# The chunk scan of a state-space layer on VectorE alone, in a one-core decoder step

## The reference, cut to what matters

```python
x_re = jnp.einsum('bngc,gpc->bngp', ug, bb_re)      # and x_im
combine: (a2r*a1r - a2i*a1i, a2r*a1i + a2i*a1r,
          a2r*b1r - a2i*b1i + b2r, a2r*b1i + a2i*b1r + b2i)
_, _, s_re, s_im = lax.associative_scan(combine, (l_re, l_im, x_re, x_im), axis=1)
y = einsum(s_re, c_re) - einsum(s_im, c_im)
```

## Time and profile before

| | |
|---|---|
| median of 3 runs | 2636.78 us |
| lowest and highest run | 2634.36 and 2637.1 us |
| profiled execution, first to last instruction (span) | 2638.2 us |
| mean granted TensorE clock | 0.945 of full speed |
| TensorE matmuls busy | 2385.0 us (90%) |
| VectorE busy | 1067.1 us (40%) |
| ScalarE busy | 816.8 us (31%) |
| GpSimd busy | 221.8 us (8%) |

### The profile page before, as it was taken

How to read it: one execution, slowest core, us unless ns; L and a number is a source line. 1 busy time by engine, 2 the same in 40 slices (tenths; PEclk the granted TensorE clock), 3 DMA queues, 4 the chain that set the end, 5 groups by cost and what they waited for, 6 DMA issues and landing times.

```text
span 2638.2 us, 46341 instructions
## 1 busy us (share of the span) xinstructions
PE 2385.0 (90%) x19286; PEld 2155.6 (82%) x19286; DVE 1067.1 (40%) x1547; ACT 816.8 (31%) x1145; POOL 221.8 (8%) x324
## 2 busy tenths in 40 slices
PE   6999997928998999998899999798996768999999
PEld 5999996724698999998799999754774448999998
DVE  4333324784534433323433332355363222434422
ACT  3443222302323434322334322222343212434311
POOL 2000001363200000000000000000002410000000
PEclk9999997967998999999899999899798988999999
DMA  3323332000032332332233333101003522233332
GB/s 91 96 87 94 102 88 55 1 0 6 2 84 70 88 95 88 104 90 54 66 96 87 95 96 88 33 21 35 11 18 88 156 78 73 72 95 87 101 94 78
DMA packets 361265, 188.87 MB, mean 72 GB/s; under 512 B 39772, under 2 KB 357338, under 8 KB 361154
## 3 DMA queue, kind: packets, MB, share of 16 engines
q1 hardware_dynamic: 354624, 176.91, 23.5%
q0 software_dynamic: 5104, 8.90, 1.2%
q10 hardware_dynamic: 1426, 1.46, 0.2%
HBM read 184.21 MB, written 3.02 MB: 71 GB/s over the span
## 4 chain that ended last, share of the span: by engine, by line
PE 63%; DVE 4%; SPq 4%; issue 2%; ACT 1%; DMA 0%; POOL 0%; DVEq 0%; ACTq 0%
PE ps L1371 51%; PE ps L1691 2%; PE ps L1380 2%; PE ps L1786 1%; PE ps L1759 1%; SPq L356 1%; SPq L357 1%; SPq L351 1%; DVE ta L917 1%; PE ps L1743 1%; DVE xl L904 1%; PE ps L1589 1%; DVE rstc L1217 1%; PE ps L1393 1%; PE ps L1762 1%
## 5 line engine op out<-in xcount | busy, mean ns | idle before, releaser
L1371 PE MATMUL ps<-xh,wh 128*128 128x260 f32 x3296 | 873.7, 286 | 23.7 <-DVE xl L904 20.9
L1371 PE MATMUL ps<-xl,wh 128*128 128x260 f32 x3296 | 864.5, 284 | 0.0
L1371 PE MATMUL ps<-xh,wl 128*128 128x260 f32 x3296 | 667.4, 284 | 0.0
L1371 PEld LDWEIGHTS ps<-xh,wh 128*128 128x128 f32 x3296 | 627.2, 190 | 32.8 <-issue 20.0
L1371 PEld LDWEIGHTS ps<-xl,wh 128*128 128x128 f32 x3296 | 626.1, 190 | 0.0
L894 DVE TENSOR_TENSOR wl<-raw,wh 128x1024 fp32r<-128x1024 f32 (+1 forms) x208 | 274.6, 1320 | 746.1 <-ACT wh L536 746.1
L1371 PEld LDWEIGHTS ps<-xh,wl 128*128 128x128 f32 x3296 | 512.2, 190 | 0.0
L536 ACT ACTIVATE wh<-raw 128x1024 fp32r<-128x1024 f32 (+1 forms) x208 | 236.5, 1137 | 662.6 <-PE ps L1371 662.6
L1371 PE MATMUL ps<-hh,wh 128*128 128x260 f32 x1408 | 370.4, 284 | 0.0
L1371 PE MATMUL ps<-hl,wh 128*128 128x260 f32 x1408 | 367.4, 282 | 0.0
L1371 PE MATMUL ps<-hh,wl 128*128 128x260 f32 x1408 | 283.3, 282 | 0.0
(11 more groups left out here) (348 smaller groups left out, 2429.0 us busy)
## 6 DMA issues: line engine op xcount, KB each, us to landing
raw<-ffn_w_gate SPq DMA_DIRECT2D x88, 512.0 KB, 3.9
raw<-ffn_w_up SPq DMA_DIRECT2D x88, 512.0 KB, 3.9
raw<-ffn_w_down SPq DMA_DIRECT2D x64, 704.0 KB, 4.6
cb<-cache_ckv SPq DMA_DIRECT2D x72, 128.0 KB, 2.5
cb<-cache_ckv POOLq DMA_DIRECT2D x56, 128.0 KB, 2.6
raw<-s_w_glu_v SPq DMA_DIRECT2D x8, 512.0 KB, 4.1
raw<-s_w_glu_g SPq DMA_DIRECT2D x8, 512.0 KB, 4.0
raw<-mla_w_o SPq DMA_DIRECT2D x8, 512.0 KB, 4.0
```

Of the source, the lines that this page charges most:

```text
L1371: got = mm(ps[0:width, bank + half, 0:HALF], w[par_][:, k * width:k * width + width], src[:, k0 + k, half * HALF:half * HALF + HALF], star ...
```

## The change

GpSimd no longer scans any pairs. VectorE scans all 32 pairs in one call, with the same 21 steps of four instructions, each now twice as wide. GpSimd's wait for tile 3 is gone with its scan, and it goes from `mu` directly to the wait for all tiles and the sample tokens' step. VectorE's waits and the semaphore counts stay as they are.

```diff
-SCAN_T = 4
...
             dve.wait_ge(s_mu, 1)
             dve.wait_ge(s_xe, KD)
-            chunk_scan(own, tt, pr, QP * SCAN_T, NPAIR, s_sn)
+            chunk_scan(own, tt, pr, 0, NPAIR, s_sn)
...
             pool.wait_ge(s_mu, 1)
-            pool.wait_ge(s_xe, SCAN_T)
-            chunk_scan(own, T, gtmp, 0, QP * SCAN_T)
-
-
             pool.wait_ge(s_xe, KD)
             pool.wait_ge(s_ev, 1)
```

## The result

| | before | after |
|---|---|---|
| median of 14 runs each | 2636.94 us | 2646.41 us |
| lowest to highest | 2634.36 to 2640.81 | 2639.85 to 2650.24 |
| profiled execution: device time, span | – , 2638.2 | 2641.32, 2639.7 |

The ratio is 1.003, 95% interval 1.002 to 1.0039: 7.9 us slower (5.3 to 10.3), where 8.7 was forecast. The medians alone are 9.5 apart. The runs of one kernel lie 6 to 10 us apart, so the stage is read from the traces and the total from the medians.

The account below looks back on a forecast made before the run. VectorE's scan was taken to bound the state-space stage, its end carrying over one to one. Start 539.7 + scan 59.1 + contention 3.6 = 602.4 against 593.7, 8.7 us later: 2645.5 us, range 2640.5 to 2652.0.

Parts of the forecast that it names:

- The loop: Input loop: without GpSimd's scan the tiles keep 10.05 us and VectorE's scan starts 6.5 us earlier, at 539.7.
- the 7.5 of TensorE alone: Input loop: the bound if TensorE's time alone set the scan's start, 538.7 instead of 546.2.
- The width: VectorE's scan: 6.35 ns per element of a step, steps of 3.90, 1.05 and 3.49 us, 59.1 us in all.
- Rival A: VectorE's scan: extra elements cost only the contiguous 1.04 ns, scan ends at 594.1, no change, or 586.5 if stronger; 5%.
- The contention: Start of VectorE's scan: GpSimd's sample step now runs beside the first two steps and costs them 3.6 us.
- B: Start of VectorE's scan: the sample step hides without loss, 5.1 us later in all, 2641.9 us; 7%.
- C: Start of VectorE's scan: full blocking by GpSimd's sample step, 6.7 us instead of 3.6, 2648.6 us; 10%.
- What costs nothing: GpSimd's sample step ends at about 546, more than 50 us before the scan ends, so its lateness is covered.
- The clock: TensorE's granted clock, rising in the first taps: unchanged place, 0 us; bounds 2.5 saved to 9 more.
- a later stage getting shorter would prove it wrong: Stages behind the scan: a later one that shortens by what the scan lost would make the prediction wrong.

Follow-up runs that it names:

- e1: Kernel before, with GpSimd's half scan waiting for all eight tiles instead of tile 3; 2650.11 us in one run.
- e3: Changed kernel without the sample tokens' state step on GpSimd (sn set to zero); scan on VectorE 59.4 us, 2633.43 us in one run.
- v1: Changed kernel with the chunks in xs reordered so the scan walks runs of neighbouring elements; 2644.77 us, 1.0028 to the kernel before.
- e2: Changed kernel with VectorE scanning pairs 16 to 31 alone, pairs 0 to 15 left out; scan 39.7 us, 2617.88 us in one run.
- v6: Kernel before with the sample step's early part moved ahead, contiguous operands in VectorE's scan, and GpSimd scanning 12 pairs from tile 2; 2631.59 us, ratio 0.9976.
- v7: Kernel before with the sample step's early part moved ahead, contiguous operands in VectorE's scan, and GpSimd scanning 8 pairs from tile 1; 2629.32 us, ratio 0.9962.

## Why the prediction was right

Forecast 2645.5 us in a range of 2640.5 to 2652.0, measured 2646.41. The +8.7 us rested on three terms. Each was measured in the changed kernel and again by an edit that makes or removes it alone. The numbers in brackets below are those of the prediction's parts.

| term | forecast | changed kernel | alone |
|---|---|---|---|
| input loop without GpSimd's scan | -6.5 | -6.5 (52.1 to 45.5) | -6.5 (e1) |
| clean scan of 32 pairs | 59.1 | 59.3 (62.6 less 3.3) | 59.4 (e3) |
| sample step beside it | +3.6 | +3.3 | +3.3 (e3 against after) |
| sum, against 47.5 | +8.7 | +8.6 | |

*The loop* (1). The 10.05 us period, taken from the starts of tiles 4 and 5, held to the end. (Tile 5 starts 2.4 us after GpSimd's scan did, so the rows did not yet prove it undisturbed; the new trace and e1 do.) Taking 6.5 rather than the 7.5 of TensorE alone was right.

*The width* (2). Steps were forecast at 3.90, 1.05 and 3.49 and measured at 3.93, 1.05 and 3.50. The line through 32 and 224 elements held at 512. Rival A, with steps of 3.27 and 3.00, is excluded by these steps, and v1 shows what it had mixed up: its price per element, 1.04 ns, is right for contiguous operands, and these are not.

*The contention* (3). 3.6 came from two steps of which the first also stood 0.5 us beside GpSimd's scan; without that scan e2 has 3.3 for steps of the same width. B (0) and C (6.7) are excluded by e3. The Trainium skill's rule of an exclusive lock (SBUF — State Buffer, section "SBUF: two separate sides") would have the two take turns, one whole instruction at a time. Measured, VectorE lost 3.3 us and GpSimd 4.3 (9.4 against 5.1). In those 9.4 us the two did 6.1 (9.4 less 3.3) and 5.1 us of clean work, 11.2 together, more than turns would allow. The measurement decides: both are slowed, neither is blocked throughout.

*What costs nothing* (4). GpSimd's sample step ended at 550.06 and not near 546, since it too was slowed. It was still 53 us ahead of the scan's end and cost nothing by its own lateness.

*The clock* (5). I had put 0 with a span of -2.5 to +9. From the scan's end to the first `ta` it is 36.9 us after and 37.8 before: 0.9 given back. But the clock did not rise once only, in the taps. The windows of TensorE in the changed kernel:

```profile
620.00:624.00 4.00, 1.37 (x3) 0.93 0.00 0
624.00:628.00 4.00, 4.00 (x5) 0.50 0.00 0
628.00:632.00 4.00, 4.00 (x40) 0.70 0.00 0
```

It rose near 620, behind the turned matrices, with TensorE mostly idle, and fell again. That rise fell on the powers ahead of the taps, and the 0.9 us came there: from the scan's end to the first tap it is 22.2 us after and 23.1 before, and the second group of powers takes 2.89 us instead of 3.78. For good it rose during the taps, 5 us into them as before, so the unchanged place that I took held in this trace. I had no reason for that place, and that 0 was near is luck. Over the traces with this stretch unchanged (all but v1) it takes 36.2 to 37.9 us.

*The total.* 7.9 us (5.3 to 10.3) by ratio, where the stage's 8.6 less the 0.9 given back make 7.7. That this reaches the end in the median but not in the profiled execution was not foreseen: the prediction said that a later stage getting shorter would prove it wrong, and in that one execution the attention did, most of it by its clock.

## What to carry to other kernels

When work moves from one engine to another, price three things apart: what the giver's absence frees in the stages beside it, what the taker's wider instructions cost at the rate of their own access pattern (two shapes of the same line give it), and which instructions now fall side by side. Here the split of a serial scan was worth more than the 6.5 us of contention it caused. All on one engine was not best, and neither clearly was half and half: with a quarter on GpSimd, done before the other begins, the stretch was shortest by 1.6 us, which the totals can't tell from the other splits. And before dividing strided work, look whether it need be strided: contiguous scratch, with an idle engine doing the scattered store, gave 8.6 us, as much as the whole change lost.

## What the hardware showed unexpectedly

- A `tensor_tensor` of fp32 on VectorE with one operand in steps of 8 elements costs 1.79 ns per element, contiguous 1.04 (1071 and 688 ns at 512). At 64 elements of the second phase (stride of a row) it is 269 against 225.
- TensorE is slower too with a moving operand in steps of 8 elements: 32.1 us busy instead of 16.0 for 1024 matmuls of 64 columns, 299 ns each instead of 219.
- GpSimd and VectorE side by side: GpSimd's six instructions 9.4 us instead of 5.1, VectorE's loss 3.3. Beside narrower instructions (e2) they take 6.8, and VectorE's loss is again 3.3.
- TensorE's granted clock fell within a product ahead of which it had waited, 3.12 us in v6 and 2.31 in v7: 6.56 and 5.41 us for 16 matmuls instead of 3.72. In the kernel before the same 16 took 5.41 in tile 5. In these traces a tile that came late cost TensorE time of its own besides.
- With the order of work unchanged, the attention stage took 7.2 us less in one execution than in another, 5.7 of them in two stretches in which the granted clock was higher. A single execution is no measure for a change of 8 us in 2640.
